# Expert gathers of a PEER layer: from 128 tokens and one expert per slot to 32 tokens and four experts

## The reference

```
q = (hb @ w_query).reshape(t, 8, 2, 128)
s = einsum('thpc,hpnc->thpn', q, sub_keys)          # 2 x 128 keys per head
v1, i1 = top_k(s[:, :, 0], 16); v2, i2 = top_k(s[:, :, 1], 16)
best, pos = top_k(v1[..., :, None] + v2[..., None, :], 16)
experts = (i1 * 128 + i2) at pos                    # 16 of 16384 per head
gate = softmax(best)
act = gelu(einsum('thkd,td->thk', expert_u[experts], hb))
out = einsum('thk,thkd->td', gate * act, expert_v[experts])
```

## Time and profile before

| | |
|---|---|
| median of 3 runs | 1307.79 us |
| the profiled execution, first to last instruction | 1307.2 us |
| PE busy | 1138.1 us, 87% |
| DVE busy | 768.2 us, 59% |
| ACT busy | 396.5 us, 30% |
| POOL busy | 291.4 us, 22% |
| gathered on q0 | 268.45 MB, 36864 packets |
| mean granted clock of PE | 0.984 |

### The profile page before, as it was taken

The page is one execution under the profiler, slowest core; times in us unless marked ns, Lnnn a source line. Parts: engine busy times, 40 slices in busy tenths (PEclk is TensorE's granted clock), DMA queues, the critical chain, the costliest instruction groups (busy, mean ns, idle before and its releaser), DMA issues.

```text
span 1307.2 us, 16265 instructions
## 1 busy us (share of the span) xinstructions
PE 1138.1 (87%) x5852; PEld 700.4 (54%) x5852; DVE 768.2 (59%) x1984; ACT 396.5 (30%) x1104; POOL 291.4 (22%) x275
## 2 busy tenths in 40 slices
PE   7999999999989998877777677779999999877897
PEld 4887889755544554332222233227878875332342
DVE  4687876989667766677767776443842516211112
ACT  2313532345323343333333233223521423000012
POOL 0000000444434344434444334420030000000000
PEclk9999999999999999999999999999999999988999
DMA  9934464899999999999999999998321476999996
GB/s 383 374 131 161 180 237 195 335 423 421 421 421 422 420 420 422 421 420 415 422 405 422 422 412 406 421 385 345 143 81 50 193 306 256 428 425 423 426 419 260
DMA packets 62971, 446.78 MB, mean 342 GB/s; under 512 B 6832, under 2 KB 7216, under 8 KB 13872
## 3 DMA queue, kind: packets, MB, share of 16 engines
q0 software_dynamic: 36864, 268.45, 49.7%
q1 hardware_dynamic: 25600, 175.97, 33.6%
q10 hardware_dynamic: 432, 1.40, 0.3%
HBM read 444.74 MB, written 1.05 MB: 341 GB/s over the span
## 4 chain that ended last, share of the span: by engine, by line
PE 51%; DMA 34%; DVE 9%; ACT 3%; issue 2%; SPq 1%; POOL 0%; DVEq 0%; ACTq 0%
DMA wring<-uv_in,arena 16%; PE bank L2830 12%; DMA arena<-uv_in,arena 9%; PE bank L2667 7%; DMA wring<-moe_in 4%; PE bank L2928 4%; DVE arena L2102 4%; PE bank L3178 3%; PE bank L3194 2%; PE bank L3136 2%; PE bank L2791 2%; PE bank L2559 2%; DMA arena<-moe_in 2%; PE bank L2925 2%; PE bank L3164 1%
## 5 line engine op out<-in xcount | busy, mean ns | idle before, releaser
L2830 PE MATMUL bank<-wring,arena 128*128 128x512 f32 x512 | 241.1, 606 | 53.5 <-ACT arena L1210 53.4
L2830 PE MATMUL bank<-arena 128*128 128x512 f32 x512 | 239.0, 612 | 53.1 <-ACT arena L1210 50.0
L921 POOL DMA_INDIRECT arena<-uv_in,arena x128 | 148.6, 1161 | 393.6 <-DVE arena L1976 231.5
L2102 DVE CUSTOM_DVE_ANT_0 arena<-wring,arena 128x1024 f32<-128x1024 f32 x128 | 156.8, 1225 | 90.0 <-DMA wring<-uv_in,arena 89.6
L2102 DVE CUSTOM_DVE_ANT_0 arena<-arena 128x1024 f32<-128x1024 f32 x128 | 156.7, 1225 | 87.9 <-DMA arena<-uv_in,arena 86.4
L2830 PEld LDWEIGHTS bank<-arena 128*128 128x128 f32 x512 | 94.3, 193 | 186.2 <-issue 101.6
L2830 PEld LDWEIGHTS bank<-wring,arena 128*128 128x128 f32 x512 | 90.8, 191 | 164.4 <-ACT arena L1210 84.3
L921 POOL DMA_INDIRECT wring<-uv_in,arena x128 | 128.4, 1003 | 202.2 <-PE bank L2830 192.6
L1202 ACT ACTIVATE arena<-arena 128x2 f32<-128x2 f32 x127 | 26.0, 205 | 398.2 <-DVE arena L2102 397.3
L2667 PE MATMUL bank<-wring,arena 128*128 128x256 f32 x448 | 98.5, 379 | 0.0
L2667 PEld LDWEIGHTS bank<-wring,arena 128*128 128x128 f32 x448 | 84.4, 190 | 11.9 <-issue 0.8
(11 more groups left out here) (509 smaller groups left out, 1582.7 us busy)
## 6 DMA issues: line engine op xcount, KB each, us to landing
wring<-stream_in SPq DMA_DIRECT2D x61, 1024.0 KB, 7.2
wring<-moe_in SPq DMA_DIRECT2D x14, 2048.0 KB, 17.8
arena<-moe_in SPq DMA_DIRECT2D x12, 2048.0 KB, 18.7
arena<-moe_in SPq DMA_DIRECT2D x23, 1024.0 KB, 18.7
wring<-moe_in SPq DMA_DIRECT2D x12, 1024.0 KB, 13.9
arena<-stream_in SPq DMA_DIRECT2D x6, 1024.0 KB, 6.9
arena<-moe_in SPq DMA_DIRECT2D x7, 512.0 KB, 8.1
wring<-moe_in SPq DMA_DIRECT2D x5, 512.0 KB, 8.2
```

Of the source, the lines that this page charges most:

```text
L921: pool.indirect_dma_start(G[j], None, uv_d, src).then_inc(gathered[j], 16)
L2102: v.tensor_tensor_reduce(out=junk, in0=G[j][:, 0:D], in1=h2[:, t, :], scale=1.0, scalar=0.0, op0=ALU.mult, op1=ALU.add, accum_out=dots[:, ...
L2830: ins = mm(bank[1 + 2 * tile + c][:, :], diag[:, j, :], G[j][:, D + c * 512:D + (c + 1) * 512], start=begins and j == 0, stop=False, skip_ ...
```

## The change

A slot now holds four experts of 32 tokens. Slot n, with token quarter n mod 4, holds in partitions 32k to 32k+31 the rows of four experts k of the 32 tokens of that quarter; four slots together hold what four slots held before. So:

- Indices and gates, computed one token per partition, must be brought into that layout. DVE writes them masked by quarter into `spread_in`, PE (`spread`) collects them with `pick32` (four stacked 32 x 32 identities), four matmuls into bank 7, and DVE (`spread_out`) copies to `expert` and `gates`. POOL's gathers wait for that (`top_ready`).
- The tokens must stand in every quarter of the partitions. PE (`repeat_tokens`) multiplies the turned tokens of a quarter by `repeat`, eight matmuls of 512 columns per tile, each copied to `h2` by ACT (`tokens_repeated`). h2 now holds the four quarters of one tile only; for tile 1 it is written over at the tile boundary, behind the last rows of tile 0.
- `diag` is 128 x 32, and a slot's product goes to 32 rows of the bank, that is to one of four groups of 32 columns of the array. `weighted_rows` takes four slots at a time: the first 512 columns of all four, then the second, which increments `slot_used`. ACT takes the dots of four slots at a time (PAIR = 4); `last_weights` now takes the last four singly.
- PE's loops in tile 1 are written out. turn_tokens(1) moves to half unit 15, key_scores(1) ahead of turn_tokens(0). Some buffers move, a semaphore is merged.

```diff
-        pick = tiny.take(8)
+        pick32 = tiny.take(QROWS)
+        pick = pick32[:, 0:8]
+        quarter_of = tiny.take(QUARTERS)
+        repeat = tiny.take(QUARTERS, QROWS)
...
-        PAIR = 2
+        PAIR = 4
...
-        h2 = m2.take(NT, D)
+        h2 = m2.take(QUARTERS, D)
...
-        diag = m2.take(GS, P)
...
+        spread_in = m2.take(2, QUARTERS, TOPK)
...
+        diag = m2.take(GS, QROWS)
...
+        by_token = [keyS1[:, 4:8].rearrange("p h c n -> p (h c n)"), qT.rearrange("p a b t -> p (a b t)")]
...
-            pool.wait_ge(first_here, 1)
+            pool.wait_ge(top_ready, 1)
...
                     if n == GS:
-                        pool.wait_ge(top_ready, 1)
+                        pool.wait_ge(top_ready, 2)
                     elif i == 0 and unit > 0:
-                        pool.wait_ge(top_ready, unit + 1)
+                        pool.wait_ge(top_ready, 2 * unit + 2)
                     if n >= GS:
                         pool.wait_ge(slot_used, n + 1 - GS)
...
-                for g in (2 * t, 2 * t + 1):
-                    act.wait_ge(tokens_turned, g + 1)
-                    nc.scalar.activation(h2[:, t, (g % 2) * 512:(g % 2 + 1) * 512],
-                                         bank[(7, 0)[g % 2]][:, :], ACT.Copy).then_inc(tokens_out, 1)
+                for half in range(2):
+                    act.wait_ge(tokens_turned, TURNED * t + half + 1)
+                    nc.scalar.activation(by_token[t][:, half * 512:(half + 1) * 512], bank[(0, 5)[half]][:, :], ACT.Copy)\
+                        .then_inc(tokens_out, 1)
+
+            def tokens_repeated(t, quarter):
+
+                if t == 1:
+                    act.wait_ge(dot_done, SLOTS - QUARTERS + quarter + 2)
+                for half in range(2):
+                    act.wait_ge(tokens_turned, TURNED * t + 2 * quarter + half + 3)
+                    nc.scalar.activation(h2[:, quarter, half * 512:(half + 1) * 512],
+                                         bank[(0, 5)[half]][:, :], ACT.Copy).then_inc(tokens_out, 1)
...
             gate_exp(0)
+            scores_out(1)
             tokens_turned_out(0)
-            scores_out(1)
+            for quarter in range(QUARTERS):
+                tokens_repeated(0, quarter)
...
                 for q in range(PAIR):
                     nc.scalar.activation(weight[:, at + q:at + q + 1], gelu[:, at + q:at + q + 1], ACT.Copy,
                                          scale=gates[:, first + q:first + q + 1]).then_inc(gelu_step, 1)
                 for q in range(PAIR):
                     act.wait_ge(gelu_step, done + (q + 2))
-                    nc.scalar.activation(diag[:, at + q, :], ident, ACT.Copy,
+                    nc.scalar.activation(diag[:, at + q, :], pick32, ACT.Copy,
                                          scale=weight[:, at + q:at + q + 1]).then_inc(diag_ready, 1)
 
             def last_weights():
...
                 for half in range(2):
                     n_half = 2 * unit + half
-                    for g in range(GS // PAIR):
-                        if (n_half, g) == (2 * UNITS - 1, GS // PAIR - 1):
+                    for g in range(GS // 2):
+                        if (n_half, g) == (2 * UNITS - 1, 2):
                             last_weights()
-                        else:
-                            weights(unit, half, g)
+                        elif g % 2 == 0:
+                            weights(unit, half, g // 2)
+                        if n_half == 2 * PH - 1 and g == 0:
+                            tokens_turned_out(1)
+                        if n_half == 2 * PH - 1 and g >= 2:
+                            for quarter in (2 * (g - 2), 2 * (g - 2) + 1):
...
+                dve.wait_ge(spread_done, 1)
+                v.tensor_copy(expert[:, r], bank[7][:, SPREAD:SPREAD + 8]).then_inc(top_ready, 1)
...
-                ins = v.tensor_copy(expert[:, unit * TOPK + lo:unit * TOPK + lo + n], posf[:, 0, r])
+                ins = v.tensor_tensor(by_quarter(spread_in[:, 0, :, r]), bc(fours(posf[:, 0, r]), 3, QUARTERS),
+                                      bc(bc(quarter_of, 1, n // 4), 1, QUARTERS), ALU.mult)
                 if unit == 0 and lo == 0:
-                    ins.then_inc(first_here, 1)
-                    dve.wait_ge(first_here, 1)
+                    ins.then_inc(spread_ready, 1)
...
-                v.tensor_scalar(best, best, gsum, None, ALU.mult).then_inc(top_ready, 1)
+                mark(v.tensor_scalar(best, best, gsum, None, ALU.mult))
+                settle()
+                v.tensor_tensor(by_quarter(spread_in[:, 1]), bc(fours(best), 3, QUARTERS),
+                                bc(bc(quarter_of, 1, TOPK // 4), 1, QUARTERS), ALU.mult).then_inc(spread_ready, 1)
+
+            def spread_out(unit):
+
+                lo = 8 if unit == 0 else 0
+                at = unit * TOPK
+                dve.wait_ge(spread_done, unit + 2)
+                v.tensor_copy(expert[:, at + lo:at + TOPK], bank[7][:, SPREAD + lo:SPREAD + TOPK]).then_inc(top_ready, 1)
+                v.tensor_copy(gates[:, at:at + TOPK], bank[7][:, SPREAD + TOPK:SPREAD + 2 * TOPK]).then_inc(top_ready, 1)
...
-            dve.wait_ge(tokens_out, 2)
             dve.wait_ge(keys_done, 2)
+            SPREAD_OUT = {(0, 1): 0, (0, 11): 1, (1, 8): 2}
...
-                if unit == PH:
-                    dve.wait_ge(tokens_out, 4)
...
-                        v.tensor_tensor_reduce(out=junk, in0=G[j][:, 0:D], in1=h2[:, t, :], scale=1.0,
+                        if n % SLOTS < QUARTERS:
+                            dve.wait_ge(tokens_out, TURNED * t + 2 * (n % SLOTS) + 4)
+                        v.tensor_tensor_reduce(out=junk, in0=G[j][:, 0:D], in1=h2[:, j % QUARTERS, :], scale=1.0,
                                                scalar=0.0, op0=ALU.mult, op1=ALU.add,
                                                accum_out=dots[:, j:j + 1])\
                          .then_inc(dot_done, 1)
...
+                        if (unit, i) in SPREAD_OUT:
+                            spread_out(SPREAD_OUT[unit, i])
+                        if 2 <= unit < UNITS - 1 and i == 1:
+                            spread_out(unit + 1)
...
 
                 if t == 0:
                     pe.wait_ge(h2_ready, KD)
-                for g in (2 * t, 2 * t + 1):
-                    if g >= 2:
-                        pe.wait_ge(tokens_out, g - 1)
-                    transposes(pe, bank[(7, 0)[g % 2]],
-                               [h2T[:, 4 * (g % 2) + k, t * P:(t + 1) * P] for k in range(4)])\
+                for half in range(2):
+                    if t == 1:
+                        pe.wait_ge(q_out, len(Q_STEPS))
+                    transposes(pe, bank[(0, 5)[half]], [h2T[:, 4 * half + k, t * P:(t + 1) * P] for k in range(4)])\
                         .then_inc(tokens_turned, 1)
 
-            def weighted_rows(first, slots=range(GS), begins=False):
-
-                for j in slots:
-                    pe.wait_ge(diag_ready, first + (j + 1))
+            def repeat_tokens(t, quarters):
+
+                for quarter in quarters:
+                    own = slice(quarter * QROWS, (quarter + 1) * QROWS)
+                    for half in range(2):
+                        pe.wait_ge(tokens_out, TURNED * t + 2 + max(0, 2 * quarter + half - 1))
+                        mm(bank[(0, 5)[half]][:, :], repeat[own].rearrange("p k j -> p (k j)"),
+                           by_token[t][own, half * 512:(half + 1) * 512], start=True, stop=True).then_inc(tokens_turned, 1)
+
+            def weighted_rows(first, pairs=range(GS // PAIR), begins=False):
+
+                for b in pairs:
                     for c in range(2):
-                        ins = mm(bank[1 + 2 * tile + c][:, :], diag[:, j, :],
-                                 G[j][:, D + c * 512:D + (c + 1) * 512], start=begins and j == 0, stop=False,
-                                 skip_group_check=True)
-                    ins.then_inc(slot_used, 1)
+                        for j in range(PAIR * b, PAIR * (b + 1)):
+                            if c == 0:
+                                pe.wait_ge(diag_ready, first + (j + 1))
+                            own = slice(j % QUARTERS * QROWS, (j % QUARTERS + 1) * QROWS)
+                            ins = mm(bank[1 + 2 * tile + c][own, :], diag[:, j, :],
+                                     G[j][:, D + c * 512:D + (c + 1) * 512], start=begins and j < QUARTERS, stop=False,
+                                     skip_group_check=True)
+                            if c == 1:
+                                ins.then_inc(slot_used, 1)
+
+            def spread(nth, n=2):
+
+                pe.wait_ge(spread_ready, nth)
+                for k in range(QUARTERS):
+                    ins = mm(bank[7][k * QROWS:(k + 1) * QROWS, SPREAD:SPREAD + (2 * TOPK if n == 2 else 8)], pick32,
```

(47 more changed lines are left out.)

54 lines of the change are left out of this document (33 added, 21 removed).

## The result

The changed kernel takes 1387.6 us, median of 4 runs (1385.8 to 1389.0), the kernel before on the same chip 1308.2: ratio 1.0606, 95% interval 1.0588 to 1.0624. The prediction said 1323, range 1312 to 1336. The sign was right, the size was five times too small. The profiled execution has a span of 1383.9 us where before it had 1307.2.

A forecast was written before the change was run, and what follows sets the result against it. The prediction took the bytes of one trailing DMA engine as the bound. Start 8.7, unit 1 1.5, boundary 1.5 and tail 3.8 sum to 15.5 us on the 1307.2 us span, 1322.7; it said 1323, range 1312 to 1336.

The forecast's parts named there:

- What bounds the kernel: Gather stretch: bound by the bytes of one trailing DMA engine, 2.485 us per gather; relieving PE gives nothing back meanwhile.
- Part 1: Gathers: still 256 slots of 128 rows of 8 KB, nothing removed, the stretch keeps its 636 us; gain 0.
- Part 2: Weighted rows on PE: four slots take 1.76 us instead of 7.13, some 330 us of PE disappear; worth 0 except in the tail.
- Part 3: Start of the gathers: index detour and repeats delay gathers 7 and 8, so gather 10 lands 8.7 us later; bounds 7.5 to 10.
- Part 4: Steady ring of eight slots, four handed over at once: cost 0 while the slack holds; unit 1 and the tile boundary exceed it.
- its bytes come 1.5 later: Steady hand-over: first bytes flow 1.5 us after a slot's reissue, so 6.5 (full clock) or 8.1 us (half) after the fourth landing.
- slack of +1.3 us: Steady hand-over at half clock: 9.4 us of transfers in the other four slots against 8.1 us until new bytes come.
- the rivals: Steady starvation: hand-over exceeds its slack every round, 32 us per us; 1339 at 0.5 us above, 1355 at 1; chance 0.15.
- Unit 1: Dot of gather 27, last of its four, trails its landing by 3.2 us, so four slots return late: 1.5 us, bounds 0 to 3.5.
- Boundary: Tile boundary: repeat matmuls behind the rows of slots 124 to 127 make dot 131 late: 1.5 us, bounds 0 to 4.
- Part 5: After the last dot: next block's weights, transposes and sums come later, nothing absorbs it: 3.8 us, bounds 2.2 to 4.5.
- The clock: PE's granted clock taken as half (1.2 GHz) after idle gaps; at full clock throughout the sum would be 2.8 us smaller.

The follow-up runs named there:

- pairs: The changed kernel with dots, weights and weighted rows handed over for two slots at a time instead of four; 1332.1 us, ratio 1.018.
- lone: The changed kernel with each gather (first tile) or group of four (second tile) issued only after the one before has landed; 1991 us.
- spread11: The changed kernel with DVE's copy of unit 2's spread result behind the dot of slot 11 of unit 1 instead of slot 8; 1382.8 us.
- mended: The changed kernel with hand-over by two, boundary repeats moved between the last rows, and the later spread copy of spread11; 1325.0 us, ratio 1.014.
- warm: The changed kernel with eight filler matmuls on zeros behind each half of a group's selection work in the second tile; 1369.4 us.
- mended_warm: mended with four filler matmuls on zeros behind each group of rows from the fifth half unit on, in both tiles; 1322.8 us.

## Why the prediction was wrong

**What bounds the kernel**, right: bytes by a trailing engine, with PE's 70 to 90% hidden. pairs relieves PE by 122 us (1016 busy instead of 1138), and its steady beat is 2.53 to 2.54 where before had 2.53 to 2.56.

**Part 1, bytes at no cost**: right (pairs, lone). **Part 2, PE's work**: right that it gives back nothing, too large in size: 179 us of PE's busy time went (1138 to 959.5), not 330, and the weighted rows alone lost 228 (480 to 252). 16 records take 1.92 to 2.54 us at the full clock (1.76 said), but 4.26 at half, as in the row of the hand-over above, and the repeats were added.

**Part 3, the start**: right to 0.2 us in its sum, 8.5 against 8.7, but by luck. Timelines of POOL and PE, and two windows:

```profile
230.49 1.12 POOL L931 DMA_INDIRECT arena<-uv_in,arena  x1 [230.05 <-DVE arena L1974]
...
244.04 9.94 PE L2883 MATMUL bank<-arena,tiny 32*128 32x512 f32 x16
250.00:252.00 2.00, 2.00 (x4) 0.58 (x3) 1.94 (x8) 0.75 (x2) 0.00 (x0) 0.50 0.50 205
...
253.91 5.84 PE L2789 MATMUL bank<-arena,wring 128*128 128x128 f32 x32
...
259.68 1.92 PE L2894 MATMUL bank<-arena 128*32 128x512 f32 x16
260.00:262.00 2.00, 2.00 (x20) 0.72 (x13) 1.97 (x5) 0.00 (x0) 1.21 (x1) 1.00 0.14 25
...
260.03 1.21 POOL L931 DMA_INDIRECT wring<-uv_in,arena  x1 [14.90 <-PE bank L2789]
262.36 0.94 POOL L931 DMA_INDIRECT arena<-uv_in,arena  x1 [1.13 <-PE bank L2894]
```

The repeats took 9.94 us, not 7.1, and project_out(1,3) 5.84, not 3.6: the granted clock had fallen to 0.5 there, where I had reckoned with the full one, so gather 7 came at 260.0 (258.1 said). The first rows I had put at the half clock, behind dot 3 and an idle PE. Dot 3 ended at 256.3 (259.45 said), PE was busy until 259.7 with project_out, and the rows ran at the full clock; gather 8 came at 262.4 (264 said, and 264.6 by the terms given, 259.45 + 5.1). From its issue to the landing of gather 10 it then took 11.0 us where 9.6 were reckoned. That is the failure of part 4 below; here 1.6 us too early and 1.4 us too long cancel.

**Part 4, the steady hand-over: the step that failed.** The mechanism (four slots come back late, two fours in the ring) was the right one, and the time to the reissue was right (6.5 against 6.6). The term behind it was not: "its bytes come 1.5 later", and a lag of 0.5. From issue to fourth landing I had 1.5 + 4 x 2.485 + 0.5 = 11.9 us; on average it is 15.9 in the first tile and 15.4 in the second. The slack of +1.3 us was thus a shortfall of some 2 us for each turn of the ring of two fours: in the second tile 6.55 + 15.4 = 22.0 us, in the first, where the reissue came 6.14 us after the fourth landing, 22.1, where two fours at the beat take 19.9. The two steady stretches have 25 turns, 10.5 and 15: 23 and 31 us, and the table has 22.8 and 29.9, of which the kernel before has 11.6 as well (its single longer beats), so 41.1 are new. Part of unit 1's excess is the same. Of the 3.5 to 4 us that the term lacked, lone explains 2.3 (14.2 on an empty queue); why it is longer still with transfers under way stays open. The mechanism stood among the rivals with its price, 32 us for each us, and a chance of 0.15; "a first-byte time read on an empty queue only" was named as what spoke for it. The row showed 33 GB/s, and one more window two us later, at 235.0, would have shown the full rate and the real delay.

**Unit 1**: 1.5 said, 16.7 measured. Without DVE's wait for the spread 7.2 come back (spread11), without the grouping 12.5 (pairs), without both 14.3 (mended), so the two overlap; 2.4 stay. **Boundary**: 1.5 said, 7.0 measured. The prediction put quarter 0 at 6.6 to 9 us after dot 127 and the others 1.8 us apart; dot 128 followed at 9.1 us, the next ones 2.8 us apart, and the 16 repeats took over 10 us. At the half clock, which it counted on elsewhere, its own terms gave 5.6 - 1.3 = 4.3, not 1.5.

**Part 5, the tail**: 3.8 said, 3.5 to 4.1 measured, in one trace of each; tails of one and the same code differ by 5 us (see mended), so the hit proves little. ACT's copy and PE's gates stand at 5.85 and 20.64 us behind the last dot, against 4.58 and 16.56:

```profile
964.88 1.08 ACT L1305 ACTIVATE mod_rows<-bank 128x512 f32<-128x512 f32 x2 [3.69 <-PE bank L2894]
...
968.17 5.41 PE L2984 MATMUL bank<-arena,wring 128*128 128x128 f32 x32 [1.06 <-DMA wring<-stream_in]
...
979.67 1.05 PE L2995 MATMUL bank<-arena 128*8 128x256 f32 x16 [0.73 <-DMA arena<-route_in]
```

**The clock**: half in the second tile, as said, and worth 18 us (warm), where the prediction gave it 2.8, since its effect runs through the same missing slack.

No version here beats the kernel before. With bytes as the bound, the column groups have only start, boundary and tail to change, and the best of those that compute everything, mended_warm at 1322.8, pays 10 us at the start.

## What to carry to other kernels

A ring of buffers behind a queue of transfers needs not just a free slot but enough transfers still queued when it is reissued: here about 6 us of them, two and a half gathers, for a group of four. Why 6 isn't known, so it should be measured again for other sizes. Measure the time from issue to landing on the row of a lone transfer and in the full ring, and don't take it from the first bytes. Handing over by halves of the ring leaves only one half as cover, and each us short is paid at each turn; hand over in the smallest groups that the consumer can bear (two and four were run here).
